# Alternating the items of two kinds of attention heads in the mixer of a two-layer diffusion trunk

## The reference

```python
def diff_attention(q, k, v, lam):              # 6 heads, two components c of 32 columns each
    s = jnp.einsum('bqhcd,bkhcd->bhcqk', qb, k) * DA ** -0.5
    p = jax.nn.softmax(s, axis=-1)
    w = p[:, :, 0] - lam * p[:, :, 1]
    return jnp.einsum('bhqk,bkhe->bqhe', w, v)
def softmax_attention(q, k, v):                # 6 heads, one component of 96 columns
    p = jax.nn.softmax(jnp.einsum('bqhd,bkhd->bhqk', q, k) * QK_C ** -0.5, axis=-1)
    return jnp.einsum('bhqk,bkhe->bqhe', p, v)
...
    o_a = rmsnorm(diff_attention(q_a, ka_all, va_all, lam), lw['subln_a']) * (1.0 - l_init)
    o_c = softmax_attention(q_c, kc_all, vc_all)
    o_b = b_b * conv
    y = jnp.concatenate([o_a, o_b, o_c], axis=-1) @ lw['w_out']
```

## Time and profile before

| | us |
|---|---|
| median of 3 runs | 2022.19 (2021.28 to 2024.68) |
| profiled execution, its own time | 2023.35 |
| its span | 2021.3 |
| PE busy | 1836.7 (91%) |
| DVE busy | 1407.1 (70%) |
| ACT busy | 1029.0 (51%) |
| POOL busy | 328.3 (16%) |

### The profile page before, as it was taken

One profiled execution on the slowest core, in us unless ns is written; L12 is line 12 of the kernel. 1 busy time (PEld: TensorE's weight loads), 2 busy tenths in 40 slices (PEclk: granted clock), 3 DMA queues, 4 the chain that ended last, 5 costly groups with the idle time before them and its releaser, 6 DMA issues.

```text
span 2021.3 us, 28791 instructions
## 1 busy us (share of the span) xinstructions
PE 1836.7 (91%) x11300; PEld 1638.5 (81%) x11300; DVE 1407.1 (70%) x2038; ACT 1029.0 (51%) x1401; POOL 328.3 (16%) x507
## 2 busy tenths in 40 slices
PE   5999778799999999998998678897999999999994
PEld 3987666698999999998987566696788888888883
DVE  5375885537665656646466885536888888888987
ACT  4235686625121121124235786534777777777772
POOL 0082541001000000001083530200000000000002
PEclk9999799999999999999999899997999999999997
DMA  9125300023544445421221000006999999999995
GB/s 342 57 93 189 109 1 1 22 84 115 167 157 136 156 136 167 133 82 53 70 78 48 1 1 1 2 22 250 391 399 398 409 408 387 404 388 404 377 392 218
DMA packets 112438, 366.21 MB, mean 181 GB/s; under 512 B 7456, under 2 KB 65216, under 8 KB 85936
## 3 DMA queue, kind: packets, MB, share of 16 engines
q1 hardware_dynamic: 94448, 303.50, 40.1%
q0 software_dynamic: 13536, 48.39, 6.9%
q10 hardware_dynamic: 4320, 12.49, 1.6%
HBM read 349.23 MB, written 15.12 MB: 180 GB/s over the span
## 4 chain that ended last, share of the span: by engine, by line
PE 74%; DVE 13%; ACT 7%; DMA 3%; issue 2%; POOL 0%; SPq 0%; POOLq 0%; DVEq 0%; ACTq 0%
PE PS L2446 27%; PE PS L2335 25%; PE PS L2003 5%; PE PS L2390 5%; PE PS L2427 4%; ACT E L909 3%; PE PS L2126 3%; PE PS L2091 3%; DVE NM L1354 2%; DVE KCn L1301 1%; DVE split L1637 1%; ACT PT L914 1%; DMA raw<-in_w_ada_head 1%; DVE SS L1284 1%; DVE QC L1301 1%
## 5 line engine op out<-in xcount | busy, mean ns | idle before, releaser
L2446 PE MATMUL PS<-H,split 128*128 128x320 f32 x2304 | 339.7, 309 | 1.6 <-DVE H L1901 1.6
L2446 PEld LDWEIGHTS PS<-H,split 128*128 128x128 f32 x2304 | 338.1, 188 | 3.1 <-DVE H L1901 2.3
L1088 ACT CAST split<-raw 128x2048 fp32r<-128x2048 f32 (+2 forms) x64 | 112.8, 1763 | 228.5 <-PE PS L2446 184.4
L1637 DVE TENSOR_TENSOR split<-raw,split 128x2048 fp32r<-128x2048 f32 (+2 forms) x64 | 138.1, 2162 | 123.9 <-ACT split L1088 123.7
L1548 DVE TENSOR_TENSOR msplit<-raw,msplit 128x2048 fp32r<-128x2048 f32 x82 | 187.9, 2292 | 36.4 <-ACT msplit L1045 36.4
L1548 DVE TENSOR_TENSOR split<-raw,split 128x2048 fp32r<-128x2048 f32 x82 | 186.8, 2290 | 18.1 <-ACT split L1045 18.0
L2335 PE MATMUL PS<-split,HT 128*128 128x512 f32 x816 | 195.7, 396 | 3.7 <-DVE HT L1527 2.4
L1045 ACT CAST msplit<-raw 128x2048 fp32r<-128x2048 f32 x82 | 157.0, 1914 | 69.7 <-PE PS L2335 60.0
L2335 PE MATMUL PS<-msplit,HT 128*128 128x512 f32 x816 | 191.2, 390 | 0.6 <-DVE msplit L1548 0.6
L2003 PE MATMUL PS<-split,H 128*128 128x384 f32 (+1 forms) x960 | 171.3, 340 | 12.8 <-DVE split L1637 9.5
L2003 PEld LDWEIGHTS PS<-split,H 128*128 128x128 f32 x960 | 169.4, 195 | 14.5 <-DVE split L1637 10.7
(11 more groups left out here) (352 smaller groups left out, 3035.2 us busy)
## 6 DMA issues: line engine op xcount, KB each, us to landing
raw<-in_moe_w_gate SPq DMA_DIRECT2D x55, 1024.0 KB, 7.5
raw<-in_moe_w_down SPq DMA_DIRECT2D x55, 1024.0 KB, 7.9
raw<-in_moe_w_up SPq DMA_DIRECT2D x54, 1024.0 KB, 7.3
DOTW<-in_w_ada_rows POOLq DMA_DIRECT2D x56, 512.0 KB, 4.0
raw<-in_w_ada_head SPq DMA_DIRECT2D x16, 1024.0 KB, 7.0
mraw<-in_moe_w_up SPq DMA_DIRECT2D x14, 1024.0 KB, 7.3
mraw<-in_moe_w_gate SPq DMA_DIRECT2D x13, 1024.0 KB, 7.4
mraw<-in_moe_w_down SPq DMA_DIRECT2D x13, 1024.0 KB, 7.8
```

The source lines that it names most:

```text
L1088: A.copy(split[u % 2][:, 0, 0:w], src[:, 0:w]).then_inc(S["split_hi"], 1)
L1637: V.tensor_tensor(split[u % 2][:, 1, 0:w], src[:, 0:w], split[u % 2][:, 0, 0:w].bitcast(f32), ALU.subtract).then_inc(S["split_lo"], 1)
L2446: ins = T.matmul(PS[:, 4 * (u % 2) + 2 * c + hf, 0:HALF], W[:, w, k, c * P:(c + 1) * P], A(a, k, hf), start=(k == 0 and w == 0 and a == 0) ...
```

## The change

A list of blocks now sets the order. Heads 0 and 1 come first as before. Then four blocks of ten places each hold a first-kind head (2, 3, 4, 5) and a second-kind head (6, 7, 8, 9), tile by tile in turn. Heads 10 and 11 come last. `HEAD_AT` and `TILE_AT` give a place's head and tile.

```diff
+BLOCKS = [(0, None), (1, None), (2, 6), (3, 7), (4, 8), (5, 9), (10, None), (11, None)]
+def item_list():
+    out = []
+    for a, c in BLOCKS:
+        for t in TILE_ORDER:
+            out += [(a, t)] if c is None else [(a, t), (c, t)]
+    return out
...
-K_SUM, K_ROOT, K_NORM, K_OUT = A_ITEMS + 4, A_ITEMS + 14, A_ITEMS + 16, ITEMS - NT - 1
-K_MIX = ITEMS - NT - 2
+K_SUM, K_NORM = {50: (0,), 51: (1, 2), 52: (3, 4)}, {53: (0,), 54: (1, 2), 55: (3, 4)}
+K_ROOT, K_OUT, K_MIX, K_CONV = 52, 53, 55, 58
...
+            events = ((3, ("pair", 0, 2)), (4, ("turn", 0, 2)), (4, ("pair", 1, 3)), (5, ("turn", 1, 3)),
+                      (7, ("pair", 4, 6)), (8, ("turn", 4, 6)), (8, ("pair", 5, 7)), (9, ("turn", 5, 7)),
+                      (9, ("single", 8)), (10, ("single", 9)))
...
+    put(1, (-2, 0), (-1, 0), (0, 0), (0, 1), (1, 0), (2, 0))
+    put(2, (3, 0), (4, 0), (5, 0), (5, 1), (6, 0), (7, 0))
+    put(6, (7, 1), (8, 0), (8, 1))
+    for first, (a, c) in zip(range(10, 50, 10), BLOCKS[2:6]):
+        if a + 1 < HEADS:
+            put(a + 1, *((first + k, 0) for k in (-1, 0, 1, 3, 4, 5)))
+        put(c + 1, *((first + k, 0) for k in (2, 6, 7)))
+    put(11, (49, 0), (50, 0), (51, 0))
...
-        PT = [at(f"PT{i}", [P, KEYS], OFF_H + 32256 + 2560 * i) for i in range(2)]
+        PT = [at(f"PT{i}", [P, KEYS], OFF_H + 32256 + 2560 * i) for i in range(3)]
...
-        LT = [at(f"LT{s}", [QK, (NT + KT_TILES) * P], OFF_SPLIT + s * 16384) for s in range(2)]
+        LTS = [[at(f"LT{l}_{s}", [QK, (NT + KT_TILES) * P], OFF_RAW + (LAYER_U[l] + U_OUT + 2 + s) % RAW_SLOTS * UNIT * 4)
+                for s in range(2)] for l in range(DEPTH)]
...
                 for j in range(4):
+                    if j == 2:
+                        sp.wait_ge(S["scored"], (l + 1) * SCORES)
                     load(base + U_OUT + j, w[:, :, j * 256:(j + 1) * 256], KC, 256)
...
             for k in range(-2, ITEMS + 1):
+                ahead = k + 2 < ITEMS and k >= -1 and comps_of(k + 2) == 1 and comps_of(k + 1) == 2
+                if ahead:
+                    invert(k + 1)
...
-                        if c == 0 and k >= -1 and comps_of(k + 1) == 2:
+                        if c == 0 and k >= -1 and comps_of(k + 1) == 2 and not ahead:
                             invert(k + 1)
...
                 if outputs_at(k):
+                    pe.wait_ge(S["ot_out"], l * pairs_before(ITEMS + 1) + pairs_before(k))
+                    if stored_before(k):
+                        pe.wait_ge(S["o_stored"], l * ITEMS + stored_before(k))
```

More of the change, by code:

```diff
@@ new lines, in comps_of, with outputs @@
+def comps_of(j):
+    return 2 if HEAD_AT[j] < HEADS else 1
+FIRST_SCORE = [sum(comps_of(i) for i in range(j)) for j in range(ITEMS)]
+A_INDEX = [sum(1 for i in range(j) if HEAD_AT[i] < HEADS) for j in range(ITEMS)]
+def score_of(j, c):
+    return FIRST_SCORE[j] + c
+def outputs():
+    at = {}
+    first = 0
+    for a, c in BLOCKS:
+        if c is None:
+            events = ((2, ("pair", 0, 1)), (3, ("turn", 0, 1)), (4, ("pair", 2, 3)), (5, ("turn", 2, 3)), (5, ("single", 4)))
+        else:
+            events = ((3, ("pair", 0, 2)), (4, ("turn", 0, 2)), (4, ("pair", 1, 3)), (5, ("turn", 1, 3)),
+                      (7, ("pair", 4, 6)), (8, ("turn", 4, 6)), (8, ("pair", 5, 7)), (9, ("turn", 5, 7)),
+                      (9, ("single", 8)), (10, ("single", 9)))
+        for k, (kind, *places) in events:
+            at.setdefault(first + k, []).append((kind, [first + j for j in places]))
+        first += NT if c is None else 2 * NT
+    return at
@@ L187, in outputs_at @@
+OUTPUTS = outputs()
 def outputs_at(k):
[L189 to L192, removed]
+    return OUTPUTS.get(k, [])
+STORE_ORDER = [j for k in sorted(OUTPUTS) for kind, places in OUTPUTS[k] if kind != "pair" for j in places]
+STORED = [STORE_ORDER.index(j) + 1 for j in range(ITEMS)]
 def outputs_ready(k):
-    return sum(1 for i in range(1, k + 1) if outputs_at(i))
@@ L200, in groups_of, with stored_before, pairs_before, turned_groups @@
-def groups_of(h):
-    return 6 if h < HEADS else 3
+    return sum(1 for i in OUTPUTS if i <= k)
+def stored_before(k):
+    return sum(len(places) for i in OUTPUTS if i < k for kind, places in OUTPUTS[i] if kind != "pair")
+def pairs_before(k):
+    return sum(1 for i in OUTPUTS if i < k for kind, _ in OUTPUTS[i] if kind == "pair")
+def turned_groups():
+    at = {}
+    def put(h, *steps):
+        for g, (k, place) in enumerate(steps):
+            at[k, place] = (h, g)
+    put(1, (-2, 0), (-1, 0), (0, 0), (0, 1), (1, 0), (2, 0))
[6 more added lines that the diff above has]
+    put(11, (49, 0), (50, 0), (51, 0))
+    return at
@@ L205, in groups_before, with group_place @@
+GROUPS_AT = turned_groups()
+GROUP_ORDER = [(0, g) for g in range(6)] + [GROUPS_AT[k] for k in sorted(GROUPS_AT)]
 def groups_before(h):
     return 6 * min(h, HEADS) + 3 * max(h - HEADS, 0)
+def group_place(h, g):
+    return GROUP_ORDER.index((h, g))
 def groups_at(k, place):
[L211 to L215, removed]
+    return GROUPS_AT.get((k, place))
@@ L1369, in mixer_dve @@
                     dve.wait_ge(S["o_ready"], l * outputs_ready(ITEMS) + outputs_ready(k))
-                for kind, j in outputs_at(k):
+                for kind, places in outputs_at(k):
                     if kind == "pair":
```

118 lines of the change are left out of this document (55 added, 63 removed).

## The result

The changed kernel takes 2032.42 us (median of 11 runs, 2028.38 to 2036.78); the kernel before, run beside it, 2024.42 (2021.28 to 2029.45). The ratio is 1.0041, with a 95% interval from 1.0030 to 1.0052. The forecast was 2011.8 with a range up to 2023. The profiled execution took 2033.85 us for a span of 2031.8, against 2023.35 and 2021.3: 10.5 us more.

What follows compares the result with a forecast made beforehand. Loop bound by PE, DVE and ACT waiting for one another, none full. Per layer -8.8 + 1.5 + 2.1 = -5.2, two layers -10.4: 2012.95 from the profiled 2023.35, median 1.16 lower, forecast 2011.8, range 1998 to 2023.

Steps and rivals of the forecast that it cites:

- The blocks: Four mixed blocks per layer: each ten places take 25.9 us instead of 28.1, PE busy 90%.
- The hand schedule: One mixed block worked out as five pairs between second-kind exponentials: 25.7 us, plus 0.2 for one late maximum.
- The yardstick: Old time for ten places, one head of each kind: 28.10 us; steps 7 to 47 taken as 4 x 28.10.
- Four blocks give 4 x 2.2 = 8.8: Saving in the mixed blocks of the loop: 8.8 us a layer.
- The early reciprocals: Reciprocals ahead of the second-kind maximum on DVE: cost nothing, and the maximum covers POOL's CNEG.
- Head 1: Steps 7 and 8 hold four groups instead of two, each waiting for a turn_out: 1.5 us a layer, 0.5 to 3.
- The end: Step 52 to OC transposes: 27 instead of 24 us, 3.2 more; net loss 2.1 a layer, bounds 0 and 5.
- since PE has slack exactly there: Ground for leaving the clock's cost at the end of the loop at nothing, though PE idles nearly 4 us.
- The late `w_out` loads: Units 2 and 3 issued after the last score, some 9 us before the product starts: cost 0.
- the rivals: PE bound: block 24.2, 1998 us, chance 0.20; handover eats the gain: 2022, no change 0.13; slower: 0.12.
- slower: Rival: values in odd steps wait behind a PT copy, block 28.0, layers lose 6.4 together: 2028.6 us, chance 0.12.
- the sum: Per layer -8.8 + 1.5 + 2.1 = -5.2, two layers -10.4, against the profiled 2023.35: 2012.95 us.

Runs made afterwards that it cites:

- experiment 2: The control: kernel before, old order of items, with only the end of the loop scheduled as in the changed kernel; 2032.73 us, ratio 1.0041.
- Experiment 6: Changed kernel with w_out cast in step 46 and head 6's three groups in steps 2, 4, 6, turning other values; 2022.89 us, ratio 0.9995.
- Experiment 10: Changed kernel with w_out cast in step 46, mix_turns behind the score, three groups instead of four in steps 7 and 8; 2023.90 us, ratio 0.9999.
- experiment 9: Kernel before with mix_turns moved behind the step's score on PE and mix_hi behind the exponentials on ACT; 2034.74 us, ratio 1.0054.
- run 7: Changed kernel's code with all heads plain, old root and normalisations, cast in step 46, head 6's groups in steps 7, 8, 9; 2037.30 us, ratio 1.0070.
- experiment 8: As run 7, but with head 6's three groups back in steps 25, 26 and 27; 2033.37 us, ratio 1.0049.
- experiment 3: Changed kernel with only the cast of the first w_out unit moved, from step 53 to step 46; 2026.34 us, ratio 1.0009.

## Why the prediction was wrong, step by step

**The blocks: the mechanism right, its size wrong.** Forecast 25.9, measured 26.98, 26.70 and 26.58. The hand schedule can be checked pair by pair. ACT's exponentials of the second kind in one block, by their starts (their pairs by hand: 6.7, 3.6, 6.1, 4.7 and 4.6):

```profile
299.19 0.80 ACT L976 ACTIVATE E<-PS,NM 128x640 f32<-128x640 f32 x1
...
305.93 0.80 ACT L976 ACTIVATE E<-PS,NM 128x640 f32<-128x640 f32 x1
...
309.46 0.38 ACT L976 ACTIVATE E<-PS,NM 128x128 f32<-128x128 f32 x1
...
315.79 0.80 ACT L976 ACTIVATE E<-PS,NM 128x640 f32<-128x640 f32 x1
317.92 0.79 ACT L976 ACTIVATE E<-PS,NM 128x640 f32<-128x640 f32 x1 [1.08 <-DVE NM L1424]
...
321.09 0.80 ACT L976 ACTIVATE E<-PS,NM 128x640 f32<-128x640 f32 x1 [0.18 <-DVE NM L1424]
...
325.89 0.80 ACT L976 ACTIVATE E<-PS,NM 128x640 f32<-128x640 f32 x1
```

6.74, 3.53, 6.33, 5.30 and 4.80. Four agree within about 0.2; the pair at a block's start is 0.6 long. DVE ahead of it shows what the schedule left out:

```profile
315.61 0.96 DVE L1435 SCALAR_TENSOR_TENSOR E<-E,CNEG 128x640 f32<-128x640 f32 x1
316.49 0.46 DVE L1408 TENSOR_SCALAR OC<-PS,RC 128x64 f32<-128x64 f32 x2
316.88 0.27 DVE L1408 TENSOR_SCALAR QA<-PS,RC 128x64 f32<-128x64 f32 x1
317.07 1.54 DVE L1424 TENSOR_REDUCE NM<-PS 128x1 f32<-128x640 f32 x2
```

A combination and three stores stand ahead of the maximum for which ACT then idles 1.08. That is read from the trace; a version without it wasn't run.

**The yardstick: wrong as well.** The gain was 4 x (28.1 - 25.9). But the 112.3 of the earlier trace rows holds the root, whose 1.1 I had seen and booked at the end of the loop, not here. Without it (experiment 2) the old order runs at 27.8 per ten places, so even the measured block of 26.7 saves 1.1, not 2.2. That 112.32 came out as 4 x 28.10 was luck: head by head the trace of the kernel before has 15.13, 15.12, 15.11, 13.96, 12.98, 12.97, 12.99 and 14.06. The last holds the root, 1.08, and the fourth, on the border of the two kinds, is 1.15 shorter than a first-kind head, which hid it. Experiment 6 gives the sum as the prediction counts it, head 6's groups apart: 4.35 a layer instead of 8.8. This step, "Four blocks give 4 x 2.2 = 8.8", is the largest error, 4.45 us a layer: some 3.4 of it the block (26.75 in the mean for 25.9, four times) and 1.1 the yardstick.

**The early reciprocals: right** that they hide `CNEG`; without them a block takes 30.5. They cost next to nothing: in the pair at the block's start DVE's reciprocals wait 1.09 for the exponential (320.09), and the maximum behind them starts 1.38 after its score (318.85 to 320.23), where 1.28 is usual.

**Head 1: outside its bounds.** Forecast +1.5 with bounds 0.5 and 3; measured 4.27 in layer 0 (111.19 against 106.92) and 4.28 in layer 1. I priced the waits of single groups. I did not follow head 6's first score, which stands behind the last `turn_out` in PE's order, nor the fall of the clock behind it. Experiment 10's layer 1 is the same crowd, slightly thinned, at full clock: 18.77 against 16.48, so some 2.3 is the crowd, of which PE's own work is 0.7; what is left of the 4.3 went with the clock, 0.92 in the entry, and with the fourth group.

**The end: undersized.** Forecast +3.2 between the transposes of step 52 and those of `OC`, or 2.1 net of the root's 1.1, with bounds 0 and 5. Measured on that stretch: +6.3 and +6.4, net 5.2 and 5.3, outside the bounds. From step 47 on it is +4.28 and +5.92, net 3.2 and 4.9. The places of the stalls were right: table loads, then cast, then the remainder ahead of the maximum of item 57. Two sizes were not. The remainder took 3.09 instead of 2.28, beside POOL's gain. And the clock, which I left at nothing "since PE has slack exactly there", is most of the loss: 4.45 of the 6.3 are PE's busy time, 16.48 to 20.93 for the same 135 matmuls, while its idle time grew by 1.9, less than the 3.2 of my hand schedule. The Trainium skill, "TensorE: Matmul & The Clock Gate", Part 1, which has the slow clock as the default and activity as what holds it off, was what I had set against my reading of the rows. The trace sides with the Trainium skill: both layers ran their end at 0.88, and at 0.85 in experiment 2. My ground for setting it aside, that layer 1 of the kernel before kept its clock behind the same root, rested on a single stretch.

**The rest.** The late `w_out` loads cost nothing, as forecast: the third cast starts at 422.40, 16.0 us behind the loop's end and after ACT has waited 10.09 for PE, the same as in the earlier trace rows. Of the two stated signs of being wrong, "if the blocks are over 27.2, or if the end of the loop costs more than 5 a layer", the first was not met (26.98 at most) and the second was, on the stretch that the prediction named. Of the rivals none described what happened: the result came near "slower" at 2028.6, but by other terms. Its block was to be 28.0, and the measured ones ran at 26.7. Per layer, forecast: -8.8 + 1.5 + 2.1 = -5.2. Measured against the control: blocks -4.35, entry +4.3, root's move and the end together +3.2 and +4.9, and steps 2 to 7 -0.5 and +0.5: +2.7 and +5.3. Between the loops 2.5 us came on top, 1.45 ahead of the first, and 1.4 came back behind the second, in stretches whose computing the change leaves as it was (below). In all the profiled execution came out 20.9 us above the 2012.95 of the sum: 8.9 from the blocks and their yardstick, 5.6 from the entry, 3.9 from the end, and 2.6 from outside the loops, for which the sum has no term.

## What to carry to other kernels

Price a saving against a control in which everything else of the change is already done; a term booked in one stretch (here the root) must be taken out of the yardstick of the other. When work is reordered, look first at the borders, where the old pattern hands over to the new one: the steady part gave 3 to 4.5 us a layer, the entry took 4.3 and the end 4 to 6. Slack of PE is no reason to put the clock at nothing: in the end of the loop 4.45 of 6.3 us were the clock. And one long wait can be dearer than several short ones: in experiment 9 the work behind a wait of 3.57 ran at half the clock, and the end took 41.7 instead of 38.0 to 39.8.

## What the runs showed of the hardware that was not expected

**Less work, longer time.** With three groups (some 1.5 us of PE's work, by run 7's layer 1) taken out of steps 25 to 27, steps 22 to 32 were longer, 29.54 and 28.45 instead of 27.28 in both layers, and the granted clock was 0.88 and 0.94 instead of 1.00 (experiments 7 and 8, one profile of each). One pair of values in each of the two stretches took 2.40 and 2.27 instead of 1.31.

**The clock has several outcomes for the same work.** The projections before layer 1's loop, from the first `CN` transposes to the values of step 2, are unchanged in all kernels. They took 53.6 or 53.7 us in five of them (before, and experiments 2, 7, 9 and 10) and 55.3 to 56.1 in the seven others, the changed kernel among them. Two of the twelve, layer 1 of the kernel before and of the changed one:

| kernel | stretch | PE busy | clock |
|---|---|---|---|
| before | 53.58 | 36.00 | 0.78 |
| changed | 55.28 | 39.30 | 0.72 |

PE's busy time differs by 3.3; DVE's is 42.30 in both. It is not the order of the heads: experiment 10 is mixed and has 53.58, experiment 8 is plain and has 55.26. What decides it stays open. For reading results it means that a loop's gain of 2 us can be hidden by a stretch that nobody changed.

**DVE and GpSimd side by side.** The `w_out` remainder takes 2.28 alone and 3.09 beside the gain on POOL, whose two instructions take 4.25 there and 2.20 with the cast moved away (experiment 3's trace). Of the two it is the second, which starts inside the remainder: 3.04 instead of 0.99, ending 0.85 behind it. The Trainium skill, "SBUF — State Buffer", section "Who interferes with whom", states that a DVE instruction with two SBUF inputs contends with a GpSimd instruction that reads SBUF. Both kinds are as it says and the trace agrees: 0.8 us on the one, 2.0 on the other.
